# A forget-gate recurrence: ten blocks made one, with token-major sums and GpSimd taking both differences

## The reference

```python
def step(S, xs):
    qc, kc, vc, fc = xs
    b = jnp.cumsum(fc, axis=1)
    b_mid = b[:, CHUNK // 2 - 1:CHUNK // 2]
    b_last = b[:, -1:]
    A = jnp.einsum('bthd,bshd->bhts', qc * jnp.exp(b - b_mid), kc * jnp.exp(b_mid - b))
    A = jnp.where(mask, A, 0.0)
    o = (jnp.einsum('bhts,bshe->bthe', A, vc)
         + jnp.einsum('bthd,bhde->bthe', qc * jnp.exp(b), S))
    S_new = (S * jnp.exp(b_last[:, 0])[..., None]
             + jnp.einsum('bshd,bshe->bhde', kc * jnp.exp(b_last - b), vc))
    return S_new, o
```

## Time and profile before

| | us |
|---|---|
| median of 3 runs | 3593.79 (3592.45 to 3594.01) |
| the profiled execution's own time | 3587.6 |
| its span | 3585.9 |
| the stage of `hgrn_heads` with `end_aside` in it | 2564.8 to 2668.6 |

### The profile page before, as it was taken

One profiled execution on the slowest core, in us unless ns is written; L12 is line 12 of the kernel. 1 busy time (PEld: TensorE's weight loads), 2 busy tenths in 40 slices (PEclk: granted clock), 3 DMA queues, 4 the chain that ended last, 5 costly groups with the idle time before them and its releaser, 6 DMA issues. The chain is left out here.

```text
span 3585.9 us, 54305 instructions
## 1 busy us (share of the span) xinstructions
PE 3289.4 (92%) x20646; PEld 2841.2 (79%) x20646; DVE 2146.1 (60%) x4081; ACT 1456.4 (41%) x2274; POOL 41.7 (1%) x66
## 2 busy tenths in 40 slices
PE   6987899999999898999999999699889999979897
PEld 4844799998888677999997888488656787867797
DVE  4523489875777735699776788523673433244553
ACT  3312444444555434444444555323333332233443
POOL 0000000000000000000000000000120000000000
PEclk8988999999999999999999999799997999979999
DMA  5575576556888644676657787432453332321453
GB/s 186 157 237 191 183 219 202 173 177 186 242 242 242 197 130 153 195 206 183 176 176 222 242 242 241 133 96 65 166 193 96 102 99 88 94 61 52 123 166 123
DMA packets 225065, 596.61 MB, mean 166 GB/s; under 512 B 27424, under 2 KB 97440, under 8 KB 224576
## 3 DMA queue, kind: packets, MB, share of 16 engines
q1 hardware_dynamic: 220656, 588.17, 53.8%
q10 hardware_dynamic: 4176, 5.29, 0.5%
HBM read 558.16 MB, written 35.19 MB: 165 GB/s over the span
## 5 line engine op out<-in xcount | busy, mean ns | idle before, releaser
L2528 PE MATMUL ps<-h_split,split_layer 128*128 128x256 f32 x6144 | 773.1, 285 | 10.9 <-DVE split_layer L2317 10.9
L2528 PEld LDWEIGHTS ps<-h_split,split_layer 128*128 128x128 f32 x6144 | 746.5, 192 | 14.2 <-DVE split_layer L2317 14.2
L2674 PE MATMUL ps<-split_layer,h_split 128*128 128x512 f32 x3072 | 702.1, 391 | 13.9 <-DVE h_split L2658 13.9
L2674 PEld LDWEIGHTS ps<-split_layer,h_split 128*128 128x128 f32 x3072 | 580.4, 189 | 135.2 <-DVE split_layer L2641 14.3
L800 PE MATMUL ps<-h_parts_ffn,split_ffn 128*128 128x512 f32 (+1 forms) x2112 | 380.6, 341 | 21.2 <-DVE h_parts_ffn L273 12.0
L800 PEld LDWEIGHTS ps<-h_parts_ffn,split_ffn 128*128 128x128 f32 x2112 | 329.6, 191 | 73.7 <-issue 23.1
L2317 DVE TENSOR_TENSOR split_layer<-ring,split_layer 128x1024 fp32r<-128x1024 f32 x256 | 311.6, 1219 | 79.6 <-ACT split_layer L2456 78.0
L742 DVE TENSOR_TENSOR split_ffn<-ring,split_ffn 128x1024 fp32r<-128x1024 f32 x132 | 161.1, 1225 | 255.9 <-ACT split_ffn L724 247.1
L2641 DVE TENSOR_TENSOR split_layer<-ring,split_layer 128x1024 fp32r<-128x1024 f32 x256 | 313.7, 1225 | 0.0
L2464 ACT ACTIVATE kept_layer<-ps 128x256 f32<-128x256 f32 x256 | 98.4, 384 | 459.0 <-PE ps L2528 458.9
L2623 ACT ACTIVATE split_layer<-ring 128x1024 fp32r<-128x1024 f32 x256 | 267.5, 1045 | 4.5 <-PEq L485 4.5
(11 more groups left out here) (590 smaller groups left out, 3782.5 us busy)
## 6 DMA issues: line engine op xcount, KB each, us to landing
ring<-in_experts SPq DMA_DIRECT2D x512, 512.0 KB, 3.8
ring<-in_mod SPq DMA_DIRECT2D x96, 512.0 KB, 4.7
ring<-in_ada SPq DMA_DIRECT2D x96, 512.0 KB, 4.3
ring<-in_ffn_in SPq DMA_DIRECT2D x88, 512.0 KB, 3.6
hidden_layer<-kept_layer SPq DMA_DIRECT2D x256, 128.0 KB, 2.0
x_sb<-hidden_layer SPq DMA_DIRECT2D x256, 128.0 KB, 3.8
ring<-in_ffn_out SPq DMA_DIRECT2D x44, 512.0 KB, 3.6
ring<-in_peer_q SPq DMA_DIRECT2D x32, 512.0 KB, 3.6
```

What stands on the lines that cost most here:

```text
L2528: ins = nc.tensor.matmul(ps[:, 4 + j % 2, 0:T], w[:, part, c], self.hsplit[:, moving, k, :], start=(k == 0 and n == 0), stop=(k == KT - 1 ...
L2674: ins = nc.tensor.matmul(ps[:, 2 * t + h, :], wsplit(j, a)[:, t * P:(t + 1) * P], w[:, b, h * 512:(h + 1) * 512], start=(j == 0 and n == 0 ...
```

## The change

The ten blocks become one, with semaphores for each handover. Within it:

- GpSimd takes both differences and all four products with keys and queries, six instructions an item; VectorE keeps the scan, the masked copy (now one instruction of 512 columns, not four of 128) and the chain. The score tile is cleared twice in all, by GpSimd, one tile for each direction.
- The carried terms turn around: the decayed queries of a chunk (128x32) are the stationary operand and the state (128x128) moves, and the result is 32 tokens by 128 features. TensorE waits for states in groups of three or four. So bank 6 holds sums by token; once per head ScalarE copies it to `kept`, TensorE transposes it (`turn_head`) and ScalarE copies the head out.
- Nine modulation groups are inside, one ahead of the first item and one in each of the eight; `mlstm` takes a fifth, ahead of its last totals. `end_aside` has none left.

The diff, cut to its core:

```diff
-        for n in range(len(items) + 2):
-            front = items[n] if n < len(items) else None
-            back = items[n - 1] if 0 < n <= len(items) else None
-            ready = items[n - 2] if n >= 2 and items[n - 2][1] == 1 else None
...
-                    @block.gpsimd
-                    def _(pool):
-                        pool.wait_ge(exps.sem, exps.n + 1)
-                        if back:
-                            nc.gpsimd.tensor_tensor(e_inv, e_inv, k(fh, fd), ALU.mult)
-                            nc.gpsimd.tensor_tensor(e_mid, e_mid, q(fh), ALU.mult)
-                        nc.gpsimd.tensor_tensor(e_b, e_b, q(fh), ALU.mult).then_inc(self.pool_done.sem, 1)
...
-                            ins = v.copy_predicated(att[:, tile(j)], masks[bd].bitcast(U32), ps[:, 0, tile(j)])
-                        ins.then_inc(att_done.sem, 1)
...
-                            nc.tensor.matmul(sum_bank[:, tile(j)], value[:, j, head], att[:, tile(j)],
-                                             start=(bd == 0 and j == 0), stop=False, skip_group_check=True)
-                        for c in range(1, NC):
-                            pe.wait_ge(states.sem, states0 + c)
-                            t = slice(order[c] * HCHUNK, (order[c] + 1) * HCHUNK)
-                            nc.tensor.matmul(sum_bank[:, t], state[:, order[c - 1], :], p_b[:, t], start=False,
-                                             stop=(bd == 1 and c == NC - 1), skip_group_check=True)
-                            if c == NC // 2:
-                                self.aside_products(pe, min(at0 + 4, at1), at1)
...
+            @block.gpsimd
+            def _(pool):
+                for d in range(2):
+                    ins = g.memset(att[d], 0.0)
+                ins.then_inc(cleared.sem, 1)
+                for t, (h, d) in enumerate(items):
+                    e_mid, e_inv, e_b, e_last, dec = factors[t % 2]
+                    pool.wait_ge(scanned.sem, at[scanned] + t + 1)
+                    if t >= 2:
+                        pool.wait_ge(turned.sem, at[turned] + t - 1)
+                        pool.wait_ge(scored.sem, at[scored] + t - 1)
+                    g.tensor_tensor(ch(e_mid), ch(b), wide(mid[d]), ALU.subtract).then_inc(mids.sem, 1)
+                    g.tensor_tensor(ch(e_last), wide(last[d]), ch(b), ALU.subtract).then_inc(lasts.sem, 1)
+                    pool.wait_ge(exps.sem, at[exps] + 5 * t + E_INV)
+                    g.tensor_tensor(e_inv, e_inv, k(h, d), ALU.mult).then_inc(factored.sem, 1)
+                    pool.wait_ge(exps.sem, at[exps] + 5 * t + E_LAST)
+                    g.tensor_tensor(e_last, e_last, k(h, d), ALU.mult).then_inc(factored.sem, 1)
+                    pool.wait_ge(exps.sem, at[exps] + 5 * t + E_MID)
+                    g.tensor_tensor(e_mid, e_mid, q(h), ALU.mult).then_inc(factored.sem, 1)
+                    g.tensor_tensor(e_b, e_b, q(h), ALU.mult).then_inc(factored.sem, 1)
...
+                    v.copy_predicated(tiled(att[d]), masks[d].bitcast(U32).unsqueeze(1).broadcast_to([P, NT, P]),
+                                      tiled(ps[:, 0, :])).then_inc(masked.sem, 1)
...
+                front(0)
+                for n in range(N):
+                    if n + 1 < N:
+                        front(n + 1)
+                    choose(n)
+                    chain(n)
...
+                exponentials(0)
+                for n in range(N):
+                    h, d = items[n]
+                    keys(n)
+                    if d == 0 and h:
+                        keep_sums(h - 1)
+                    if n + 1 < N:
+                        exponentials(n + 1)
+                    if d == 0 and h:
+                        keep_head(h - 1)
+                    self.keep_row(act, first + n)
+                keep_sums(HEADS - 1)
+                keep_head(HEADS - 1)
+                self.keep_row(act, first + N)
...
+                for j in range(first, first + G):
+                    self.fetch_group(sp, j)
+                    self.store_row(sp, j)
...
+                def values(n):
+                    h, d = items[n]
+                    pe.wait_ge(masked.sem, at[masked] + n + 1)
+                    for j in range(NT):
+                        ins = nc.tensor.matmul(ps[:, 6, tile(j)], att[d][:, tile(j)], value[:, j, h * P:(h + 1) * P],
+                                               start=(d == 0 and j == 0), stop=False, skip_group_check=True)
+                    ins.then_inc(valued.sem, 1)
...
+                    for c in range(c0, c1):
+                        ins = nc.tensor.matmul(ps[rows(o[c]), 6, tile(o[c] * HCHUNK // P)],
+                                               e_b[:, o[c] * HCHUNK:(o[c] + 1) * HCHUNK], state[:, o[c - 1], :], start=False,
+                                               stop=(d == 1 and c == NC - 1), skip_group_check=True)
+                    if c1 == NC:
+                        ins.then_inc(contributed.sem, 1)
...
+                self.aside_products(pe, 8 * first, 8 * first + 8)
+                turn_keys(0)
+                scores(0)
+                for n, (h, d) in enumerate(items):
+                    aside = 8 * (first + 1 + n)
+                    update(n)
+                    if d == 0 and h:
+                        turn_head(h - 1)
+                    values(n)
+                    self.aside_products(pe, aside, aside + 4)
+                    carry(n, 1, 4)
+                    carry(n, 4, 8)
+                    self.aside_products(pe, aside + 4, aside + 8)
+                    if n + 1 < N:
+                        turn_keys(n + 1)
+                    carry(n, 8, 12)
+                    carry(n, 12, NC)
+                    if n + 1 < N:
+                        scores(n + 1)
+                turn_head(HEADS - 1)
...
@@ -3484,6 +3606,7 @@
                     if h + 1 < HEADS:
                         rows(2 * h + 2)
                     totals(2 * h, range(2, NT))
+                self.aside_products(pe, 8 * (hosted0 + HEADS), 8 * (hosted0 + HEADS) + 8)
                 totals(N - 1, range(NT))
                 turn(HEADS - 1)
 
@@ -3561,8 +3684,8 @@
                     weigh(2 * h + 1)
                     if h:
                         move(h - 1)
+                    self.keep_row(act, hosted0 + h)
                     if h + 1 < HEADS:
-                        self.keep_row(act, hosted0 + h)
                         weigh(2 * h + 2)
                 move(HEADS - 1)
 
@@ -3570,9 +3693,9 @@
             def _(sp):
                 for h in range(HEADS):
                     self.fetch_group(sp, hosted0 + h)
-                    if h + 1 < HEADS:
-                        self.store_row(sp, hosted0 + h)
-        self.groups_hosted(hosted0, HEADS)
+                    self.store_row(sp, hosted0 + h)
+                self.fetch_group(sp, hosted0 + HEADS)
+        self.groups_hosted(hosted0, HEADS + 1)
         for x, n in ((rows_made, N), (scored, HEADS * NT), (capped, N), (weighed, N), (multiplied, N * NT), (summed, N),
                      (normed, N), (turned, HEADS), (moved, HEADS)):
             x.up(n)
```

230 lines of the change are left out of this document (134 added, 96 removed).

## The result

| | before | after |
|---|---|---|
| median, us | 3593.12 (3588.01 to 3594.01, 4 runs) | 3568.02 (3565.44 to 3572.03, 4 runs) |
| the profiled execution's own time | 3587.6 | 3567.96 |
| its span | 3585.9 | 3566.3 |

The ratio is 0.9934 with an interval of 0.9917 to 0.9951: faster by 18 to 30 us. The two profiled executions are 19.6 apart.

A forecast was written before the change was run, and what follows sets the result against it. VectorE was taken to bound the stage's middle before, two loops of waits after. Stage 98.6 to 81.3 (11.3 + 7 x 8.8 + 8.4), less 4.2 clock and 0.5 `mlstm`: 12.6 off 3593.8 gives 3581.2; range 3576 to 3590.

The forecast's parts named there:

- I estimate that two such falls cost time in the new block: TensorE's idle gap of about 2.1 an item lets the clock fall twice, 2.1 us each: 4.2 us lost.
- The rival with the clock held: TensorE's clock does not fall in the items: 16.8 us less, 3577.0; chance 0.25.
- `mlstm` at 0.5: The fifth group, 1.92 us, goes into an idle gap of 1.48 ahead of the last totals and costs 0.5.
- What is behind the row copy ... stays: At the stage's end, store, wait and next block after the last row copy stay at 5.2 us.
- Items 8.8: Pace of the new block's items, set by the loop of two items: 8.8 us against 10.55 before.
- The loop of one item: After the last state: four carried terms, next item's scores, updates, chain and handovers, 8.4 us an item.
- The loop of two items: Path through chain, scan, GpSimd's differences, ScalarE's row copy and TensorE: 17.4 us, 17.9 with the head's copy.
- Start 11.3, measured 12.1; end 8.4: First scan to first state takes 11.3 us; last chain's start to the end of the row copy 8.4.
- Carried terms at 0.27 for four: Four turned carried terms on TensorE overlap, 0.27 us; rival without overlap: 0.98, giving 3587.2, chance 0.14.
- GpSimd bound: Rival: GpSimd instructions at 1.76 us make items 11.6, 3599.0 in all; decides from about 1.65; chance 0.08.
- I add nothing: Weight fetches by DMA, 5.2 us a group, have room in an item of 8.8: no cost added.
- I take the difference off the median: The 12.6 us is subtracted from the median 3593.8, as the profiled execution was 6.2 below it: 3581.2.

The follow-up runs named there:

- e9: The changed kernel with GpSimd taking two extra differences an item into tiles nobody reads; median 3580.48, ratio 0.9980, stage 92.9 us.
- e1: The kernel before with only the fifth modulation group moved into `mlstm`, ahead of its last totals, ten blocks kept; median 3584.83, ratio 0.9984, stage 97.1 us.
- e4: The changed kernel with the fifth group cut in halves, four products ahead of the last totals and four behind; median 3564.27, ratio 0.9928, stage 80.7 us.
- e5: The changed kernel with ScalarE's row copy moved ahead of the next item's exponentials; median 3566.95, ratio 0.9941, stage 79.4 us.
- e7: The changed kernel with fifth group in halves, row copy ahead of the next exponentials, scores ahead of the last carried terms; median 3561.02, ratio 0.9921, stage 76.8 us.
- e3: The changed kernel with carried terms and scores times values in the form of before; median 3575.41, ratio 0.9954, stage 86.3 us.
- e11: The changed kernel as it is, run again on the chip that also ran the version with three edits; median 3571.39, ratio 0.9955, stage 80.8 us.
- e6: The changed kernel with the next item's scores ahead of the last four carried terms; median 3571.69, ratio 0.9953, stage 81.0 us.

## Why the prediction was wrong

The direction and the two loops that bound the item were right; the size was not. The forecast was 13.2 too high (3581.2, measured 3568.0). Of this the terms of the sum are 4.8, net of errors of both signs, 2.2 lies behind the stage in code that didn't change, and 6.2 is the median from which the difference was taken. The terms, in the order of their weight:

- **"I estimate that two such falls cost time in the new block": this step failed.** No window from 2581 to the end of the last item's work shows a lower clock. TensorE's gap was 1.1 to 1.4, not 2.1. In the item whose updates begin at 2604.55 it is 1.10: the item is 0.3 shorter than forecast, and TensorE's work around the gap is 0.7 longer, half of it in the two half groups with seven carried terms between them (2.93 from start to start, 2.57 in the sum). Of e9's four gaps of 3 even, two brought no fall. The term was drawn from a single gap of 1.19 ahead of a fall, too little for a rule. The rival with the clock held was the case that came, and its 16.8 is the nearest of those written.
- **`mlstm` at 0.5: failed, by 2.5 the other way.** The idle gap of 1.48 would have hidden most of the group, but only its products were counted. Its weights weren't there: the group ahead had just freed the ring, so the four fetches were issued only from 2551.81 on, and the second half came in two pairs of products at 2559.11 and 2560.34, with waits of 1.25 and 0.18, and each pair took the 1.05 that four take elsewhere. e1 shows the loss without the block, e4 removes it.
- **"What is behind the row copy ... stays": failed, by 2.5 in favour.** Taken as a constant, it was most likely a small store waiting behind 2 MB of weights. e1, which moves one group from the end into `mlstm` and nothing else, gets 2.3 of it.
- **Items 8.8, measured 8.49: mis-sized, 2.2 in all.** The loop of one item was exact (8.38 in e5, forecast 8.4). The loop of two items was too long: a difference with a stride-0 operand on GpSimd was taken at 1.27 and measured 1.04 to 1.08, 0.4 in two items. The rest was not placed.
- **Start 11.3, measured 12.1; end 8.4, measured 8.75: mis-sized, 1.2 together.** In the start the largest part is the clock: the updates, 1.47 in the sum, take 2.02, because the granted clock is 0.50 until 2580 here and came back within 2576 before. The second scan and GpSimd's second product also exclude each other: 2.21 and 2.18 instead of 1.22 and 1.27. The five GpSimd instructions take 6.66 and not 6.35, since the cheaper differences give part of that back. The 0.3 for the memsets didn't come, the prediction's only allowance for such excess. The Trainium skill ("SBUF — State Buffer", SBUF: two separate sides) has just this rule, that the two wait for each other for a whole instruction; the trace agrees in both places, 2.21 here and 2.10 in e7.
- **Carried terms at 0.27 for four: right**, 0.285 measured. Against the 0.98 of four with all columns stationary that is 3.4 times less. The rival fell; e3 shows the price of long carried terms: 6.0 for the stage. The Trainium skill ("TensorE: Matmul & The Clock Gate", Part 3: Packing small matmuls — row/col tiling) gives 2.38 times for three such tiles of 512 moving columns; the four tiles of 128 here, at 3.4 times, do no worse for each tile.
- **GpSimd bound: the mechanism is real, its price wasn't.** At 1.04 to 1.29 per instruction the change stays just short of it, e7 and e9 reach it. Its break-even of 1.65 per instruction doesn't fit its own items of 10.9: six and the scan give 10.9 at 1.61.
- **"I add nothing" for DMA: not quite right.** TensorE held by the ring was one of the signs of being wrong, and it came in small: 0.22 and 0.21 in the last item, and weight loads that waited 0.51 and 0.30 in two others. The other way round, windows at 0.50 within the items were a sign of being right and didn't come.

By terms: 12.6 + 4.2 (clock) + 2.5 (store) + 2.2 (items) - 1.2 (ends) - 2.9 (`mlstm`, 0.4 of it drift ahead of the group) = 17.4. The profiles have 19.6. The other 2.2 arises behind the stage, in code that is the same. The next products are 1.5 shorter (L399, 9.97 before and 8.47 after), those behind them 1.4 longer (L411, 12.65 and 14.02), and the next 1.3 shorter (L800 and L804, 46.57 and 45.24). The clock is low for parts of the first two in both profiles, and the same kernel took 9.64 for L399 in e11. So this is scatter between executions as far as is known, and the last 0.7 was not placed.

The step **"I take the difference off the median"** failed as well. The profiled execution of before lay 6.2 below its median, that of after on its own; with a perfect 19.6 the forecast would have been 3574.2, below the range but 6 over the result. With the terms as measured (17.4) it would have been 3576.4, just inside the range, so the terms alone don't account for the miss. Later runs of before gave medians of 3590.5, 3589.5, 3589.0 and 3587.9, and beside the last the change was 16.5 faster. So I estimate that the change is worth about 20 us, between the 16.5 and the 25.1 of the two chips, and that some 5 of the first 25 are scatter. By e1's medians, about a quarter of it comes from the move of one group and needs no one block.

## What to carry to other kernels

A gap that hides work hides only what has its data: before pricing work moved into a gap, follow its weights back to what frees their buffer. Don't carry "what stands behind" as a constant when the change moves DMA, because a small store may be waiting behind large loads. And when two loops are within 0.1 us of each other, relieving one is worth little until the other is cut too (stages: e5 0.9 shorter, e6 no shorter, both together 3.5 shorter). When a change bundles several moves, run each alone before naming its cause: here the move of one group looked like part of the one block.

## What was not expected of the hardware

- A two-input instruction of GpSimd on 128x512 took 1.04 to 1.08 where one operand repeats with stride 0 and both come from one tile, and 1.27 to 1.29 for two separate tensors.
- Four f32 matmuls with 32 stationary columns, 128 moving ones and four different row ranges of the result take 0.285 in a row; with all columns stationary and 32 moving, four take 0.85 (1.70 for eight), hardly less than the 0.98 of four with 128 moving. So with the full stationary side, fewer moving columns save little.
- A late unit of weights need not show as a wait of the matmuls. In e11 one item took 9.52, because seven passes of a half group took 1.93 instead of 1.03 at a granted clock of 1.00. The matmul row has no wait; the row of the weight loads has it. Why that unit came late is open.

```profile
2602.94 1.93 PE L1112 MATMUL ps<-ring,ed_condition_block_layer 128*32 128x512 f32 x7
2603.81 0.14 PEld L1112 LDWEIGHTS ps<-ring,ed_condition_block_layer 128*32 128x32 f32 x4 [0.77 <-DMA ring<-in_ada]
```

- A fall of the clock is not told by the gap ahead of it. In e1 it came in an item whose only gaps were 0.42 and 0.46; timeline of TensorE, and the window:

```profile
2603.08 1.16 PE L3188 MATMUL ps<-h_block_layer,arena_block_layer 128*128 128x128 f32 x8 [0.46 <-DVE h_block_layer L3120]
2606.51 1.94 PE L1108 MATMUL ps<-ring,ed_condition_block_layer 128*32 128x512 f32 x8
```

```profile
2606.00:2607.00 1.00, 1.00 (x6) 0.65 (x10) 0.93 (x3) 0.00 (x0) 1.00 (x2) 0.50 0.90 315
```

In the eleven profiles of the one block other than e9's, with gaps up to 2.1 in the items, it never fell there. What decides it stays open.
